# A two-layer encoder: one more couple of seven products in a second wide pair, weight sums in another order, and evictions moved from VectorE to ScalarE

## The chip, the cores and the metric

The kernel runs on one core of a Trainium2 chip. The metric is the device time of one execution in microseconds (us). The engines named here are TensorE (PE: matrix products into PSUM banks of 128 x 512 f32), VectorE (DVE: elementwise), ScalarE (ACT: elementwise, casts, PSUM evictions), GpSimd (POOL) and SyncE (SP: it only issues DMAs here). Each engine works through its own instructions in order; semaphores order the engines among each other.

## The reference

Two layers over 256 tokens of width 2048. The part that the change touches is the second half of each layer, a feed-forward block:

```python
x = x + rms_norm(mixed, g_mix_post)
f = jnp.square(jax.nn.relu(rms_norm(x, g_ffn_pre) @ w_up)) @ w_down   # 2048 -> 8192 -> 2048
return x + rms_norm(f, g_ffn_post)
```

Everything is f32. Ahead of it stand an input projection, dilated window attention with pooling, and an output projection.

## The kernel before, in words

**Products.** An f32 operand is split into a high part (a cast to fp32r on ScalarE) and a low part (the operand less its high part, on VectorE). Every product is then three matmuls into one bank: high by high, high by low, low by high (`three`, L870).

**Weights.** They stream from memory in slots of 128 x 1024 f32 (512 KB). SP loads a slot into one of four `raw` buffers when the low part of what was in that buffer before is made (`load_wide`, L431). ScalarE makes `w_hi` (`split_hi`, L990), VectorE makes `w_lo` (`split_lo`, L1440), both into a ring of eight slots, and TensorE uses them. So one `raw` buffer is bound up from its load to its low part, and the next load into it can't be issued before.

**The feed-forward block** is done in four groups (0 to 3) of 2048 inner columns. A group has four "units" of the up projection (each gives 512 columns for both halves of the tokens, called t = 0 and 1), and then the down projection of those 2048 rows: two "wide pairs" q = 0 and 1, each of 1024 output columns and 16 slots, one slot for each 128 rows (a k tile). Group 3 has one wide pair alone. A plain slot of a wide pair is 12 matmuls: two halves of tokens by two halves of columns by three. 

**Couples.** Two slots next to each other (two k tiles) can be done in one of two ways: as two plain slots, 24 matmuls, or as a couple with seven products in place of eight, 21 matmuls (`seven`, L880; Strassen's scheme in Winograd's form). A couple needs sums of the activations of its two k tiles (`s_sum`, then its high and low part, made once for a group: `s_sums`, `s_rest`) and sums of its weights: three differences `t_sum` of 512 columns and a fourth ("third" in the code) that overwrites the right half of the first slot in `raw`, all on VectorE (`weight_sums`, L1983). ScalarE then makes `t_hi` (1536 columns), VectorE `t_lo`. Four of the seven products gather in four shared banks (`ssa_bank`, two `t_bank`, `o_bank`) over a whole wide pair. After q = 0 VectorE moves these into `kept_sums` (copies in groups 0 and 1, additions in groups 2 and 3: `shared_sums`, L2024), and at the layer's end they are combined into `acc`. The other products gather in the four banks of `acc_pair`, which `wide_sums` (L1946, instructions at L1934 and L1937) adds, scaled by `rstd`, into `acc` after each wide pair.

**Order of work.** It is written out by hand, engine by engine. `SEVEN_AT` says at which slots of a wide pair couples start: 0, 4, 8 and 12, in both pairs. VectorE's order for one couple and its two plain slots is (`seven_lo`, L2017): weight sums, `w_lo` of two slots, `t_lo`, `w_lo` of the two plain slots. ScalarE's is: `w_hi` of the couple's two slots, `t_hi`, `w_hi` of two plain ones; its first cast of a couple waits until "third" has overwritten `raw`. TensorE waits for `w_lo` of a couple's second slot before it starts it, and for `t_lo` some matmuls later. After a second wide pair VectorE makes the low parts of the next unit's first four slots and then evicts the four banks; the next unit's first product waits for the eviction of its bank.

Of the kernel before, what the change touches and what calls it, by code (L numbers as in the profile page):

```python
# [38 lines left out]
F32 = mybir.dt.float32  # L39
# [6 lines left out]
P = 128  # L46
# [96 lines left out]
SHARED = 4  # L143

# [6 lines left out]
def seven_no(l, g, q, n):  # L151

    return ((l * WIDE_LAYER) + g * 2 + q) * len(SEVEN_AT) + n

# [11 lines left out]
def wide_done(l, g, q):  # L166

    return l * WIDE_LAYER + g * 2 + q + 1
# [8 lines left out]
def build(nc, x_in, positions, g_mix_pre, w_in, g_attn_out, w_pool, pool_scale, g_pool_out,  # L177
# [13 lines left out]
    def own(name, shape, dtype=F32):  # L191
# [65 lines left out]
    t_lo = [at(f"t_lo{n}", [P, 3, CH], F32R, low) for n, (_, low) in enumerate(r_t)]  # L257
    r_s = ((r_qkv + 36 * CH, r_qkv + 40 * CH), (r_qkv + 44 * CH, r_xg), (r_xg + 4 * CH, r_post),
           (r_post + 4 * CH, r_post + 8 * CH))
# [26 lines left out]
    rt = [own(f"rt{n}", [P, T, ROPE // 2]) for n in range(6)]  # L286
    rt_i = own("rt_i", [P, T, ROPE // 2], I32)
    pos_f = own("pos_f", [P, T])
    freq = own("freq", [P, ROPE // 2])
# [5 lines left out]
    t_bank = [nc.alloc_psum_tensor(f"t_bank{n}", [P, CH], F32) for n in range(2)]  # L295
    o_bank = nc.alloc_psum_tensor("o_bank", [P, CH], F32)
    ssa_bank = nc.alloc_psum_tensor("ssa_bank", [P, CH], F32)
# [95 lines left out]
    with nc.Block() as block:  # L393
# [3 lines left out]
        def _(sp):  # L397
# [33 lines left out]
            def load_wide(l, g, j, hu):  # L431

                for i in range(SLOTS):
                    p = i % PAIRS

                    sp.wait_ge(lo_made, (hu + i // PAIRS) * PAIRS + p + 1)
                    src = w_down[ld(l, 1), ld(g * D + K_ORDER[i] * P, P), ld(j * 2 * CH, 2 * CH)]
                    sp.dma_start(raw[:, p, :], src.rearrange("a p c -> p (a c)")
                                 ).then_inc(raw_loaded[p], 16)

            def load_group(l, g, last=False):
# [3 lines left out]
                load_wide(l, g, pair_at(g, 0), hu + 2 * CHUNKS)  # L445
                if not last:
                    load_wide(l, g, pair_at(g, 1), hu + 2 * CHUNKS + PAIR_HALVES)
                    return
# [72 lines left out]
        def _(pe):  # L521
# [163 lines left out]
            for l in range(DEPTH):  # L685
# [194 lines left out]
                def seven(g, q, n, hu, result):  # L880

                    i = SEVEN_AT[n]
                    no, s0, s1 = seven_no(l, g, q, n), i % RING, i % RING + 1
                    k0, k1 = K_ORDER[i], K_ORDER[i + 1]
                    first = n == 0
                    begin, end = first and (q == 1 or g == 0), n == len(SEVEN_AT) - 1 and q == 0
# [1524 lines left out]
```

## Time and profile before

| what | before |
|---|---|
| device time, median of 3 runs | 1889.77 us (1889.09 to 1890.19) |
| the profiled execution | 1889.38 us |
| its span, first to last instruction | 1887.3 us |
| TensorE busy | 1874.9 us, 99% |
| VectorE busy | 1497.9 us, 79% |
| ScalarE busy | 1111.4 us, 59% |
| granted TensorE clock, mean | 0.999 |

The profiled execution stands for the runs: it lies 0.4 us below their median. Busy shares are means over the whole span; the down projection's wide pairs are one of several stages, and in them the timelines of the engines are read side by side. In a timeline a length is from start to end of an instruction (or of "x2" of them in a row); the next one of the same engine can start before that end, so the cost of an instruction to its engine is the distance between two starts.

### The profile page before, as it was taken

How to read it: one execution, taken by the hardware profiler on the slowest of the kernel's cores; microseconds unless marked ns; L12 is line 12 of the kernel's file. 1: busy time of each engine (PE TensorE's matmuls, PEld its weight loads, DVE VectorE, ACT ScalarE, POOL GpSimd, SP SyncE). 2: the span in 40 equal slices, each digit the busy share in tenths (PEclk: the TensorE clock that was granted, in tenths of full speed). 3: DMA queues.
4: the chain of work that ended last, by engine and by line, in shares of the span. 5: the costliest groups of instructions: out<-in, count | busy, mean ns of one | idle time of the engine just before them, and what ended most of it. 6: DMA issues, size and time to landing. Idle time of an engine off the chain costs nothing.

```text
span 1887.3 us, 27369 instructions
## 1 busy us (share of the span) xinstructions
PE 1874.9 (99%) x9950; PEld 1672.1 (89%) x9950; DVE 1497.9 (79%) x1885; ACT 1111.4 (59%) x1485; POOL 118.5 (6%) x166
## 2 busy tenths in 40 slices
PE   9999999999999999999999999999999999999998
PEld 7988988988988998898888888889889889989987
DVE  6886657898699689788877757678977996897886
ACT  6455656855665565566554556568556655645662
POOL 3920010000000000000000000100000000000000
PEclk9999999999999999999999999999999999999999
DMA  8665366757566666767576554586676666567673
GB/s 290 201 221 181 112 201 226 236 182 255 189 198 216 214 198 195 236 202 241 210 234 225 187 168 134 170 275 194 197 236 207 195 212 221 183 207 235 221 257 124
DMA packets 170068, 390.92 MB, mean 207 GB/s; under 512 B 12161, under 2 KB 14321, under 8 KB 168433
## 3 DMA queue, kind: packets, MB, share of 16 engines
q1 hardware_dynamic: 167904, 377.58, 61.8%
q10 hardware_dynamic: 2064, 12.08, 1.7%
q8 instruction: 56, 0.92, 0.2%
q14 instruction: 44, 0.35, 0.1%
HBM read 382.53 MB, written 7.08 MB: 206 GB/s over the span
## 4 chain that ended last, share of the span: by engine, by line
PE 95%; DVE 3%; issue 1%; ACT 0%; DMA 0%; POOL 0%; DVEq 0%; POOLq 0%; ACTq 0%
PE acc_pair L573 25%; PE acc_pair L578 13%; PE acc_pair L539 8%; PE acc_pair L540 8%; PE acc_pair L541 8%; PE acc_pair L874 7%; PE acc_pair L873 7%; PE acc_pair L872 7%; DVE w_lo L1445 1%; PE t_bank L874 1%; PE t_bank L873 1%; PE t_bank L872 1%; PE o_bank L791 1%; DVE h_both L1501 1%; PE ssa_bank L872 1%
## 5 line engine op out<-in xcount | busy, mean ns | idle before, releaser
L995 ACT CAST w_hi<-raw 128x1024 fp32r<-128x1024 f32 x687 | 703.6, 1048 | 476.4 <-DVE raw L1998 190.7
L1445 DVE TENSOR_TENSOR w_lo<-raw,w_hi 128x1024 fp32r<-128x1024 f32 x687 | 827.4, 1232 | 169.0 <-ACT w_hi L995 161.8
L573 PE MATMUL acc_pair<-h_both,w_hi 128*128 128x512 f32 x2176 | 560.3, 380 | 0.2
L573 PEld LDWEIGHTS acc_pair<-h_both,w_hi 128*128 128x128 f32 x2176 | 371.4, 190 | 30.4 <-issue 0.5
L578 PEld LDWEIGHTS acc_pair<-h_both,w_lo 128*128 128x128 f32 x2176 | 327.4, 190 | 29.2
L578 PE MATMUL acc_pair<-h_both,w_lo 128*128 128x256 f32 x2176 | 330.5, 274 | 0.0
L872 PE MATMUL acc_pair<-w_hi,f_hi 128*128 128x512 f32 x504 | 191.0, 379 | 0.0
L873 PE MATMUL acc_pair<-w_lo,f_hi 128*128 128x512 f32 x504 | 191.0, 379 | 0.0
L874 PE MATMUL acc_pair<-w_hi,f_lo 128*128 128x512 f32 x504 | 191.0, 379 | 0.0
L539 PE MATMUL acc_pair<-w_hi,h_both 128*128 128x512 f32 x444 | 170.4, 384 | 1.8 <-DVE w_lo L1445 1.6
L540 PE MATMUL acc_pair<-w_lo,h_both 128*128 128x512 f32 x444 | 168.3, 379 | 0.0
L541 PE MATMUL acc_pair<-w_hi,h_both 128*128 128x512 f32 x444 | 168.3, 379 | 0.0
L539 PE MATMUL acc_pair<-w_hi,f_hi 128*128 128x512 f32 x384 | 148.0, 385 | 0.0
L540 PE MATMUL acc_pair<-w_lo,f_hi 128*128 128x512 f32 x384 | 145.5, 379 | 0.0
L541 PE MATMUL acc_pair<-w_hi,f_lo 128*128 128x512 f32 x384 | 145.5, 379 | 0.0
L2013 DVE TENSOR_TENSOR t_lo<-t_sum,t_hi 128x1536 fp32r<-128x1536 f32 x56 | 98.1, 1753 | 12.4 <-ACT t_hi L1325 12.4
L872 PEld LDWEIGHTS acc_pair<-w_hi,f_hi 128*128 128x128 f32 x504 | 95.3, 189 | 13.5
L874 PEld LDWEIGHTS acc_pair<-w_hi,f_lo 128*128 128x128 f32 x504 | 95.3, 189 | 13.5
L873 PEld LDWEIGHTS acc_pair<-w_lo,f_hi 128*128 128x128 f32 x504 | 95.3, 189 | 13.5
L2223 POOL TENSOR_TENSOR rstd<-mean_sq,minus_half 128x1 f32<-128x1 f32 (+1 forms) x16 | 13.5, 843 | 1407.8 <-DVE ss_post L1460 1135.5
L539 PEld LDWEIGHTS acc_pair<-w_hi,h_both 128*128 128x128 f32 x444 | 83.9, 189 | 15.7 <-issue 2.9
L541 PEld LDWEIGHTS acc_pair<-w_hi,h_both 128*128 128x128 f32 x444 | 83.9, 189 | 12.0
(252 smaller groups left out, 2293.8 us busy)
## 6 DMA issues: line engine op xcount, KB each, us to landing
raw<-in_w_up SPq DMA_DIRECT2D x256, 512.0 KB, 4.4
raw<-in_w_down SPq DMA_DIRECT2D x240, 512.0 KB, 5.0
raw<-in_w_in SPq DMA_DIRECT2D x128, 512.0 KB, 4.7
raw<-in_w_out SPq DMA_DIRECT2D x64, 512.0 KB, 5.3
raw_side<-in_w_down SPq DMA_DIRECT2D x16, 512.0 KB, 7.0
x_kept<-x ACTq DMA_DIRECT2D x4, 1024.0 KB, 6.2
x<-x_kept ACTq DMA_DIRECT2D x4, 1024.0 KB, 6.1
x<-in_x SPq DMA_DIRECT2D x8, 256.0 KB, 7.5
```

The lines of the kernel that those rows point to most:

```text
L539: pe.matmul(bank[:, :], xh, wh, start=begin and k == 0, stop=False)
L540: pe.matmul(bank[:, :], xh, wl, start=False, stop=False)
L541: mm = pe.matmul(bank[:, :], xl, wh, start=False, stop=end and k == 1)
L573: pe.matmul(acc_pair[b][:, m, :], w_hi[:, slot, col:col + P], x_both.rearrange("p s (a n) -> p s n a", a=2), start=(slot, k) == (0, 0), st ...
L578: mm = pe.matmul(acc_pair[b][:, m, 0:SEQ], w_lo[:, slot, col:col + P], x_hi.rearrange("p (a n) -> p n a", a=2), start=False, stop=(slot, k ...
L791: mm = pe.matmul(o_bank[:, e * SEQ:(e + 1) * SEQ], proj[:, 6 + h // 4, kt, h_cols(h % 4)], probs_t[:, e, kt, :], start=kt == 0, stop=kt == 1)
L872: pe.matmul(bank, xh, in_turn(wh), start=start, stop=False)
L873: pe.matmul(bank, xh, in_turn(wl), start=False, stop=False)
L874: return pe.matmul(bank, xl, in_turn(wh), start=False, stop=stop)
L995: act.copy(w_hi[:, half * PAIRS + p, :], raw[:, p, :]).then_inc(hi_made, 1)
L1445: dve.tensor_tensor(w_lo[:, slot, :], src[:, p, :], w_hi[:, slot, :].bitcast(F32), ALU.subtract).then_inc(lo_made, 1)
L2013: dve.tensor_tensor(t_lo[n % 2][:, :, :], t_sum[n % 2][:, :, :], t_hi[n % 2][:, :, :].bitcast(F32), ALU.subtract).then_inc(t_lo_made, 1)
```

## The change

- The second wide pair of groups 0 to 2 has five couples, at slots 0, 4, 8, 12 and 14; its k tiles come in another order. The first wide pair is as it was.
- There is a fifth set of activation sums, made in the last unit of each group.
- "Third" is now the first of the weight sums and waits for both slots to be loaded; then one sum of 512 columns, then one subtraction of 1024 columns in place of two of 512. The third of the fifth couple stands ahead of `t_lo` of the fourth.
- The four shared banks are one PSUM tensor. In groups 2 and 3 VectorE adds them with one instruction of 2048 columns, in groups 0 and 1 ScalarE copies them.
- In group 0 ScalarE evicts `acc_pair` into `acc` after both wide pairs, in place of VectorE.
- After a second wide pair VectorE evicts behind two `w_lo` of the next unit, not four.
- Some small tables share memory with a buffer.

```diff
-SEVEN_AT = (0, PAIRS, RING, RING + PAIRS)
-SEVEN_UNIT = ((1, 0), (1, 1), (2, 0), (2, 1))
-K_ORDER = (4, 5, 0, 1, 6, 7, 2, 3, 8, 9, 12, 13, 10, 11, 14, 15)
+SEVEN_AT = ((0, 4, 8, 12), (0, 4, 8, 12, 14))
+COUPLES = tuple(len(at) for at in SEVEN_AT)
+SEVEN_UNIT = ((1, 0), (1, 1), (2, 0), (2, 1), (3, 0))[:max(COUPLES)]
...
+                def first_shared(g):
+
+                    if g == 0:
+                        act.wait_ge(x_saved, 16 * T * (l + 1))
+                    act.wait_ge(t_used, 3 * seven_no(l, g, 0, COUPLES[0]) - 1)
+                    for k in range(SHARED):
+                        act.copy(kept_sums[:, 1 - pair_at(g, 0), k, :], shared[:, k, :]
+                                 ).then_inc(shared_free, 1)
...
                     if not last:
-                        for n in range(PAIR_HALVES):
-                            seven_hi(g, 1, n, hu + 12 + n, n % 2)
-                        split_hi(hu + 16, 0)
+                        wide_hi(g, 1, 0, 2)
+                        if g < T:
+                            first_shared(g)
+                        two_hi(g, 1, 2)
+                        if first:
+                            first_sums(0)
+                        wide_hi(g, 1, 4)
+                        split_hi(hu + 16, 0, (0, 1))
+                        if first:
+                            first_sums(1)
+                        split_hi(hu + 16, 0, (2, 3))
                         split_hi(hu + 17, 1)
                         return
...
-                def weight_sums(g, q, n, hu):
...
-                    dve.wait_ge(raw_loaded[0], hu * 16 + 16)
-                    dve.tensor_tensor(out[:, 0, :], top_r, top_l, ALU.subtract
-                                      ).then_inc(t_step, 1)
-                    dve.wait_ge(raw_loaded[1], hu * 16 + 16)
-                    dve.tensor_tensor(top_r, low_r, top_r, ALU.subtract).then_inc(t_third, 1)
...
-                    dve.tensor_tensor(out[:, 1, :], low_r, out[:, 0, :], ALU.subtract
-                                      ).then_inc(t_step, 1)
...
-                    dve.tensor_tensor(out[:, 2, :], low_l, out[:, 1, :], ALU.subtract
-                                      ).then_inc(t_step, 1)
+                def weight_third(g, q, n):
...
+                    for m in range(2):
+                        dve.wait_ge(raw_loaded[i % PAIRS + m], hu * 16 + 16)
+                    dve.tensor_tensor(top_r, low_r, top_r, ALU.subtract).then_inc(t_third, 1)
+
+                def weight_sums(g, q, n):
...
+                    dve.wait_ge(t_third, no + 1)
+                    dve.tensor_tensor(out[:, 0, :], top[:, c_cols(1)], top[:, c_cols(0)], ALU.add
                                       ).then_inc(t_step, 1)
...
+                    dve.tensor_tensor(out[:, 1:3, :], low, out[:, 0:1, :].to_broadcast([P, 2, CH]),
+                                      ALU.subtract).then_inc(t_step, 1)
...
+                    dst = kept_sums[:, 1 - pair_at(g, 0), :, :]
+                    dve.tensor_tensor(dst, shared[:, :, :], dst, ALU.add
+                                      ).then_inc(shared_free, SHARED)
```

**Where instructions move.** The first place is VectorE, the end of the second wide pair of group 1, from the last couple's weight sums on. In the names, `t_sum_94` and the like are buffers. Before:

```order
L1995 TENSOR_TENSOR t_sum_94<-raw 128x512 [waits raw_loaded0,t_used]
L1998 TENSOR_TENSOR raw<-raw 128x512 [waits raw_loaded1]
L2002 TENSOR_TENSOR t_sum_94<-raw,t_sum_94 128x512 [waits t_used,t_step]
L2007 TENSOR_TENSOR t_sum_94<-raw,t_sum_94 128x512 [waits t_used,t_step]
L1445 TENSOR_TENSOR w_lo<-raw,w_hi 128x1024 [waits hi_made] x2
L2013 TENSOR_TENSOR t_lo_96<-t_sum_94,t_hi_92 128x1536 [waits t_hi_made]
L1445 TENSOR_TENSOR w_lo<-raw,w_hi 128x1024 [waits hi_made] x6
L1937 SCALAR_TENSOR_TENSOR acc<-acc_pair,rstd,acc 128x512 [waits acc_done] x2
L1937 SCALAR_TENSOR_TENSOR acc<-acc_pair,rstd,acc 128x512 [waits third_done]
L1937 SCALAR_TENSOR_TENSOR acc<-acc_pair,rstd,acc 128x512 [waits w_used]
```

After, from the weight sums of the fourth couple of that pair:

```order
L2083 TENSOR_TENSOR t_sum_94<-raw 128x512 [waits t_third,t_used]
L2088 TENSOR_TENSOR t_sum_94<-raw,t_sum_94 128x1024 [waits t_used,t_step]
L1522 TENSOR_TENSOR w_lo<-raw,w_hi 128x1024 [waits hi_made] x2
L2068 TENSOR_TENSOR raw<-raw 128x512 [waits raw_loaded3,raw_loaded2]
L2095 TENSOR_TENSOR t_lo_96<-t_sum_94,t_hi_92 128x1536 [waits t_hi_made]
L2083 TENSOR_TENSOR t_sum_93<-raw 128x512 [waits t_third,t_used]
L2088 TENSOR_TENSOR t_sum_93<-raw,t_sum_93 128x1024 [waits t_used,t_step]
L1522 TENSOR_TENSOR w_lo<-raw,w_hi 128x1024 [waits hi_made] x2
L2095 TENSOR_TENSOR t_lo_95<-t_sum_93,t_hi_91 128x1536 [waits t_hi_made]
L1522 TENSOR_TENSOR w_lo<-raw,w_hi 128x1024 [waits hi_made] x2
L2009 SCALAR_TENSOR_TENSOR acc<-acc_pair,rstd,acc 128x512 [waits acc_done,acc_free0]
L2009 SCALAR_TENSOR_TENSOR acc<-acc_pair,rstd,acc 128x512 [waits w_used]
```

The fifth couple (third, `t_sum_93`, two `w_lo`, `t_lo_95`) stands in the place of two plain `w_lo`, and the four evictions come after two of the next unit's `w_lo` in place of four.

The second place is ScalarE, the end of the second wide pair of group 0 and the start of group 1's first unit. Before:

```order
L1325 CAST t_hi_92<-t_sum_94 128x1536 [waits t_step]
L995 CAST w_hi<-raw 128x1024 [waits w_used,raw_loaded2]
L995 CAST w_hi<-raw 128x1024 [waits w_used,raw_loaded3]
L995 CAST w_hi<-raw 128x1024 [waits w_used,raw_loaded0]
L995 CAST w_hi<-raw 128x1024 [waits w_used,raw_loaded1]
L995 CAST w_hi<-raw 128x1024 [waits w_used,raw_loaded2]
```

After:

```order
L1389 CAST t_hi_91<-t_sum_93 128x1536 [waits t_step]
L1022 CAST w_hi<-raw 128x1024 [waits w_used,raw_loaded0]
L1022 CAST w_hi<-raw 128x1024 [waits w_used,raw_loaded1]
L1380 ACTIVATE acc<-acc_pair,rstd 128x512 [waits acc_done,rstd_ready]
L1380 ACTIVATE acc<-acc_pair,rstd 128x512 [waits w_used]
L1380 ACTIVATE acc<-acc_pair,rstd 128x512 [waits t_used]
L1380 ACTIVATE acc<-acc_pair,rstd 128x512
L1022 CAST w_hi<-raw 128x1024 [waits w_used,raw_loaded2]
L1022 CAST w_hi<-raw 128x1024 [waits w_used,raw_loaded3]
```

There is one more `t_hi`, and four evictions (L1380) stand between the casts of slots 1 and 2 of the next unit.

The third place is VectorE in the last unit of group 1, between two uses of `acc_pair` by L1914 (after: L1991). Before:

```order
L1914 TENSOR_TENSOR act_f<-acc_pair,act_f 128x512 [waits half_taken]
L1995 TENSOR_TENSOR t_sum_94<-raw 128x512 [waits raw_loaded0,t_used]
L1998 TENSOR_TENSOR raw<-raw 128x512 [waits raw_loaded1]
L2002 TENSOR_TENSOR t_sum_94<-raw,t_sum_94 128x512 [waits t_used,t_step]
L2007 TENSOR_TENSOR t_sum_94<-raw,t_sum_94 128x512 [waits t_used,t_step]
L1924 TENSOR_TENSOR f_lo<-act_f,f_hi 128x512 [waits fhi_made,f_ready]
L1445 TENSOR_TENSOR w_lo<-raw,w_hi 128x1024 [waits hi_made] x2
L1914 TENSOR_TENSOR act_f<-acc_pair,act_f 128x512 [waits half_taken]
```

After:

```order
L1991 TENSOR_TENSOR act_f<-acc_pair,act_f 128x512 [waits half_taken]
L2068 TENSOR_TENSOR raw<-raw 128x512 [waits raw_loaded1,raw_loaded0]
L2083 TENSOR_TENSOR t_sum_94<-raw 128x512 [waits t_third,t_used]
L2088 TENSOR_TENSOR t_sum_94<-raw,t_sum_94 128x1024 [waits t_step]
L2043 TENSOR_TENSOR s_sum_106<-act_f 128x128 [waits f_ready]
L2045 TENSOR_TENSOR s_sum_106<-act_f 128x128
L2048 TENSOR_TENSOR s_sum_106<-s_sum_106,act_f 128x128 [waits s_step]
L2051 TENSOR_TENSOR s_sum_106<-act_f,s_sum_106 128x128 [waits s_step]
L2001 TENSOR_TENSOR f_lo<-act_f,f_hi 128x512 [waits fhi_made]
L1522 TENSOR_TENSOR w_lo<-raw,w_hi 128x1024 [waits hi_made] x2
L1991 TENSOR_TENSOR act_f<-acc_pair,act_f 128x512 [waits half_taken]
```

The two differences that were one after the other are one, and four small additions (`s_sum_106`) come ahead of `f_lo`, which ScalarE waits for before it makes `t_hi` of the second couple.

## Rows read from the trace of the kernel before

**Rows 1.** Page, part 1: busy us (share of the span), instructions of each engine.
```profile
PE 1874.9 (99%) x9950; PEld 1672.1 (89%) x9950; DVE 1497.9 (79%) x1885; ACT 1111.4 (59%) x1485; POOL 118.5 (6%) x166
```
**Rows 2.** Timeline of TensorE, group 1, layer 0: start and length (us), line, tiles.
```profile
543.69 0.38 PE L872 MATMUL acc_pair<-t_hi,f_hi 128*128 128x512 f32 x1
...
588.37 0.38 PE L872 MATMUL ssa_bank<-w_hi,s_hi 128*128 128x512 f32 x1
...
598.08 0.38 PE L872 MATMUL ssa_bank<-w_hi,s_hi 128*128 128x512 f32 x1
...
617.50 1.03 PE L573 MATMUL acc_pair<-h_both,w_hi 128*128 128x512 f32 x4
...
618.81 1.03 PE L573 MATMUL acc_pair<-h_both,w_hi 128*128 128x512 f32 x4
```
**Rows 3.** Timeline of VectorE, same stage; in brackets idle time before, and releaser.
```profile
541.39 0.68 DVE L1914 TENSOR_TENSOR act_f<-acc_pair,act_f 128x512 f32<-128x512 f32 x1
...
546.65 1.76 DVE L2013 TENSOR_TENSOR t_lo<-t_sum,t_hi 128x1536 fp32r<-128x1536 f32 x1 [1.54 <-ACT t_hi L1325]
...
550.86 2.35 DVE L1445 TENSOR_TENSOR w_lo<-raw,w_hi 128x1024 fp32r<-128x1024 f32 x2
553.13 1.75 DVE L2013 TENSOR_TENSOR t_lo<-t_sum,t_hi 128x1536 fp32r<-128x1536 f32 x1
554.80 2.35 DVE L1445 TENSOR_TENSOR w_lo<-raw,w_hi 128x1024 fp32r<-128x1024 f32 x2
557.07 0.68 DVE L1995 TENSOR_TENSOR t_sum<-raw 128x512 f32<-128x512 f32 x1
558.06 0.69 DVE L1998 TENSOR_TENSOR raw<-raw 128x512 f32<-128x512 f32 x1 [0.31 <-DMA raw<-in_w_down]
558.67 0.68 DVE L2002 TENSOR_TENSOR t_sum<-raw,t_sum 128x512 f32<-128x512 f32 x1
559.39 0.69 DVE L2007 TENSOR_TENSOR t_sum<-raw,t_sum 128x512 f32<-128x512 f32 x1
560.00 2.35 DVE L1445 TENSOR_TENSOR w_lo<-raw,w_hi 128x1024 fp32r<-128x1024 f32 x2
...
577.95 2.71 DVE L1937 SCALAR_TENSOR_TENSOR acc<-acc_pair,rstd,acc 128x512 f32<-128x512 f32 x4
...
583.11 2.35 DVE L1445 TENSOR_TENSOR w_lo<-raw,w_hi 128x1024 fp32r<-128x1024 f32 x2
...
592.21 2.35 DVE L1445 TENSOR_TENSOR w_lo<-raw,w_hi 128x1024 fp32r<-128x1024 f32 x2
...
599.70 0.69 DVE L1998 TENSOR_TENSOR raw<-raw 128x512 f32<-128x512 f32 x1 [0.59 <-DMA raw<-in_w_down]
```
**Rows 4.** Waits of VectorE: total us, times, longest.
```profile
DVE raw L1998 <- DMA raw<-in_w_down: 10.1, 24, 0.8
```
**Rows 5.** Timeline of VectorE, four small additions of one sum of activations, group 1.
```profile
517.44 0.29 DVE L1965 TENSOR_TENSOR s_sum<-act_f 128x128 f32<-128x128 f32 x1
...
518.50 0.68 DVE L1924 TENSOR_TENSOR f_lo<-act_f,f_hi 128x512 fp32r<-128x512 f32 x1
```
**Rows 6.** Groups of instructions by line and form: total us, mean ns.
```profile
L995 ACT CAST w_hi<-raw 128x1024 fp32r<-128x1024 f32 x687 | 703.6, 1048 | 476.4 <-DVE raw L1998 190.7 <-PE acc_pair L578 94.1 <-PE acc_pair L541 73.2
...
L1292 ACT COPY act_f<-acc_pair 128x512 f32<-128x512 f32 x60 | 35.0, 584 | 95.0 <-PE acc_pair L578 94.7
...
L1223 ACT ACTIVATE acc<-acc_pair,rstd 128x512 f32<-128x512 f32 x16 | 11.0, 685 | 3.0 <-PE acc_pair L541 3.0
...
L2035 DVE TENSOR_TENSOR kept_sums<-t_bank,kept_sums 128x512 f32<-128x512 f32 x8 | 5.1, 680 | 0.0
```
**Rows 7.** Timeline of both engines where group 2 of layer 0 ends.
```profile
777.74 2.72 DVE L1937 SCALAR_TENSOR_TENSOR acc<-acc_pair,rstd,acc 128x512 f32<-128x512 f32 x4
...
778.83 0.38 PE L874 MATMUL acc_pair<-w_hi,f_lo 128*128 128x512 f32 x1
...
779.29 1.12 PE L573 MATMUL acc_pair<-h_both,w_hi 128*128 128x512 f32 x4
```

More of the change, by code:

```diff
@@ L137, with k_order, t_buffer @@
 WIDE_LAYER = 2 * FF_GROUPS - 1
-SEVEN_AT = (0, PAIRS, RING, RING + PAIRS)
-SEVEN_UNIT = ((1, 0), (1, 1), (2, 0), (2, 1))
-K_ORDER = (4, 5, 0, 1, 6, 7, 2, 3, 8, 9, 12, 13, 10, 11, 14, 15)
+SEVEN_AT = ((0, 4, 8, 12), (0, 4, 8, 12, 14))
+COUPLES = tuple(len(at) for at in SEVEN_AT)
+LAYER_COUPLES = FF_GROUPS * COUPLES[0] + (FF_GROUPS - 1) * COUPLES[1]
+SEVEN_UNIT = ((1, 0), (1, 1), (2, 0), (2, 1), (3, 0))[:max(COUPLES)]
 SHARED = 4
+def k_order(q):
+    pairs = [4 * u + 2 * b for u, b in SEVEN_UNIT[:COUPLES[q]]]
+    plain, order = iter([k for k in range(0, KT, 2) if k not in pairs]), []
+    for i in range(0, SLOTS, 2):
+        k = pairs[SEVEN_AT[q].index(i)] if i in SEVEN_AT[q] else next(plain)
+        order += [k, k + 1]
+    return order
+K_ORDER = (k_order(0), k_order(1))
+def t_buffer(q, n):
+    return (q * COUPLES[0] + n) % 2
 def pair_at(g, q):
@@ L151, in seven_no @@
 def seven_no(l, g, q, n):
-    return ((l * WIDE_LAYER) + g * 2 + q) * len(SEVEN_AT) + n
+    return l * LAYER_COUPLES + g * sum(COUPLES) + q * COUPLES[0] + n
 def shared_done(l, g):
@@ L294, in build @@
     s_bank = [pair[:, 1, :] for pair in acc_pair]
-    t_bank = [nc.alloc_psum_tensor(f"t_bank{n}", [P, CH], F32) for n in range(2)]
-    o_bank = nc.alloc_psum_tensor("o_bank", [P, CH], F32)
-    ssa_bank = nc.alloc_psum_tensor("ssa_bank", [P, CH], F32)
+    shared = nc.alloc_psum_tensor("shared", [P, SHARED, CH], F32)
+    ssa_bank, t_bank, o_bank = shared[:, 0, :], [shared[:, 1, :], shared[:, 2, :]], shared[:, 3, :]
     sem = nc.alloc_semaphore
@@ new lines, in wide_hi @@
+                def wide_hi(g, q, begin, end=SLOTS):
+                    for i in range(begin, end, 2):
+                        two_hi(g, q, i)
+                        if i in SEVEN_AT[q]:
+                            sums_hi(g, q, SEVEN_AT[q].index(i))
+                def first_shared(g):
[5 more added lines that the diff above has]
+                                 ).then_inc(shared_free, 1)
@@ L2012, in sums_lo @@
                     dve.wait_ge(t_hi_made, seven_no(l, g, q, n) + 1)
[L2013 to L2014 removed]
+                    dve.tensor_tensor(low[:, :, :], t_sum[t_buffer(q, n)][:, :, :],
+                                      high[:, :, :].bitcast(F32), ALU.subtract
                                       ).then_inc(t_lo_made, 1)
[L2017 to L2022 removed]
@@ new lines, in couple_lo, with wide_lo @@
+                def couple_lo(g, q, i):
+                    n = SEVEN_AT[q].index(i)
+                    weight_sums(g, q, n)
+                    two_lo(g, q, i)
+                    if i + 2 in SEVEN_AT[q]:
+                        weight_third(g, q, n + 1)
+                    sums_lo(g, q, n)
+                def wide_lo(g, q, begin):
+                    for i in range(begin, SLOTS, 2):
+                        if i not in SEVEN_AT[q]:
+                            two_lo(g, q, i)
+                            continue
+                        if i - 2 not in SEVEN_AT[q]:
+                            weight_third(g, q, SEVEN_AT[q].index(i))
+                        couple_lo(g, q, i)
```

256 lines of the change are left out of this document (145 added, 111 removed).

## The prediction

> **What bounds the kernel now.** I read the page first: TensorE is busy 99% of the span [rows 1], so time goes down only as matmuls go and up only as TensorE is made to stop. In the timeline of the second wide pair of group 1, layer 0, couples of four slots start 9.71 us apart, 45 matmuls each (21 of the couple, 24 of its two plain slots), so one 512-column matmul takes 9.71/45 = 0.2158 us [rows 2]. The question is then how far ahead of TensorE its suppliers are. The timeline of VectorE gives that: a couple can start when the low part of its second slot is made, and TensorE starts 588.37 - (583.11 + 2.35) = 2.91 us after that at slot 4, and 598.08 - (592.21 + 2.35) = 3.52 us after it at slot 8 [rows 2, 3]. VectorE gains about 0.6 us per couple, and then spends it: 2.71 us of evictions per pair [rows 3]. I call this number the lead; the change spends it.
>
> The loop that sets VectorE's pace is one of latency. A slot is reloaded when its low part is made. The part of the couple's second slot ended at 550.86 + 2.35 = 553.21, and its next contents let L1998 go at 558.06: 4.85 us [rows 3]. At 592.21 + 2.35 = 594.56 and 599.70 it is 5.14 [rows 3]; I take 4.97, the mean of the four such places in this group's wide stage. L1998 waited so in 24 of its 56 runs, 10.1 us in all [rows 4]: four couples a group, in three groups and two layers.
>
> **The change part by part.** *Matmuls.* A couple is 21 matmuls where two plain slots are 24. Three groups in each of two layers get one more couple: 6 x 3 = 18 fewer, 18 x 0.2158 = 3.88 us, all on TensorE's path.
>
> *Order of the weight sums.* Before: four sums of 512 columns, the first done ahead of the second slot's landing (557.07 did not wait, 558.06 did). From landing to the end of the second low part: 560.00 + 2.35 - 558.06 = 4.29 us [rows 3]. After, the third difference comes first and waits for both landings, and the other two instructions each need the one ahead. A sum that needs the one ahead follows after 0.72 (558.67 to 559.39), otherwise after 0.60 [rows 3]. A subtraction of 1024 columns is issued in about 2.27/2 = 1.14 (560.00 plus two low parts to the next instruction; the same spacing follows from 550.86 to 553.13) [rows 3]. So 0.72 + 0.72 + 1.14 = 2.58 in place of 0.60 + 0.60 + 0.72 + 0.61 = 2.53: no gain, and all of it stands behind the landing. From landing to the second low part: 2.58 + 2.35 = 4.93, so 0.64 later at each couple that waits for its landing. The cycle becomes 4.97 + 4.93 = 9.90 us against TensorE's 9.71: the lead now shrinks by 0.19 a cycle instead of growing.
>
> The Trainium skill, "VectorE: DVE Perf Modes", section on the TRN2 errata, gives an fp32 tensor_tensor (N + 151)/0.96 ns, 691 at 512 columns, which the 0.68 to 0.69 of the rows agrees with [rows 3]. By it two subtractions in one save 158 ns a couple; eight couples would give the tightest place 8 x (0.158 + 0.05) = 1.7 us more lead, and the time would be near the second rival's. The rows speak against it: durations overlap there, and what counts is the spacing, 0.60 and 1.14, which saves 0.06, and a second handover of 0.12 eats it.
>
> *A fifth sum of activations* in each group's last unit: four small additions, 518.50 - 517.44 = 1.06 us of VectorE, and a low part of 0.60 [rows 5]. The instructions behind it are delayed by 1.06. TensorE uses the bank that L1914 frees: that ended at 541.39 + 0.68 = 542.07 and TensorE comes at 543.69, so 1.62 shrinks to 0.56 [rows 2, 3], hidden, but nearly not. The t_lo at 546.65 waits 1.54 for ScalarE, which waits for f_lo of the same unit [rows 3]; so most of the 1.06 gets through, and I take 1.0. The low part of 0.60 stands in that wait.
>
> *The lag at slot 4 of the second pair*: 1.0, and 0.05 and 0.64 and 0.64 for three couples, and 0.05 for its own sums: 2.38. Three groups then differ.
> Group 2: the shared banks are added by one instruction of 2048 columns. No row shows one; three rows of 512, 1024 and 1536 are spaced 0.60, 1.14 and 1.67 (553.13 to 554.80) [rows 3], so 2.2, against four of 0.60. Bounds are 1.67 and 2.72 (four rows of 0.680 [rows 6]). It gains 0.2. Lead: 2.91 - 2.38 + 0.2 = 0.73, then 0.54, then 0.35.
> Group 1: ScalarE copies the shared banks, four of 0.584 [rows 6], right behind t_hi. VectorE is spared 2.40, but its next low parts wait for casts that stand behind the copies: from the third difference on ScalarE needs about 7.1 (two casts, t_hi, four copies, a cast, less overlaps) where VectorE needs 6.5, so 0.6 comes back. Lead: 0.73 - 0.2 + 1.8 = 2.33, 2.14, 1.95.
> Group 0: as group 1, and the four evictions of 2.71 go to ScalarE too [rows 3]. Lead above 4.
>
> *The fifth couple* has no plain slots behind it. From the end of the fourth couple's low parts VectorE needs the third difference (0.60), t_lo (1.67), the add (0.72), the subtraction (1.14) and two low parts (2.27): 6.40. TensorE has 21 matmuls, 4.53. The lead falls by 1.87: to -1.52 in group 2, 0.08 in group 1, above 2 in group 0. A stop adds handover and a slow start: the second of four evictions ended at 777.74 + 2.72 - 1.32 = 779.14, TensorE went on at 779.29, and its first four matmuls took 1.12 where 1.03 is usual [rows 2, 7]: 0.15 + 0.09 = 0.24. Group 2 stops for 1.52 + 0.24 = 1.76, group 1 for 0.16.
>
> *The evictions behind it.* Before, they wait for TensorE (779.29 is the one stop of this kind, 0.34, and it goes) [rows 7]. Now t_lo of the fifth couple (1.67), two low parts (2.27) and two evictions (1.32) end 5.26 after the low part that let TensorE go; with 0.15 the next unit can start at 5.41, and TensorE is there at 0.24 + 4.53 = 4.77. Stop 0.64, with the slow start 0.73, in groups 1 and 2.
> Group 0: ScalarE evicts all four between the casts of slots 1 and 2 of the next unit. The last product is there 0.38 - 0.22 = 0.16 after TensorE could go on, then two evictions 2 x 0.685 less 0.10 of overlap, a cast 1.05 [rows 6], a low part 1.23 (half of 2.35 and a little): 3.71. TensorE wants the third slot 2 x 1.31 = 2.62 later (617.50 to 618.81 for one) [rows 2]. Stop 1.09 + 0.24 = 1.33.
>
> *At no cost*: group 3's fifth sum, in the same last unit, and no fifth couple there: its lag of 2.3 stands against the lead of 2.9. If that cover is short, group 3 costs up to 1 us a layer. Tables moved in memory and the order of k tiles change addresses alone; SP's queue waits for the same low parts.
>
> **Sum.** Per layer 1.33 + (0.16 + 0.73) + (1.76 + 0.73) = 4.71, two layers 9.42. Against the profiled execution of 1889.38 us (a span of 1887.3 and 2.1 around it; 0.4 under the median of the runs, 1889.77): 1889.38 - 3.88 - 0.34 + 9.42 = 1894.6.
>
> **Rivals.** *The stops don't come*: if the evictions and copies given to ScalarE leave VectorE ahead everywhere, 1889.38 - 3.88 - 0.34 = 1885.2. For it: VectorE gains 0.6 a couple now, and 2.4 to 5.1 us of its work a pair go elsewhere in half of the groups. Against it: 6.40 against 4.53 at the fifth couple, and group 0's stop, which rests on no lead at all. Chance 0.13.
> *The lead holds*: landings at 4.5 us, since the transfers meet fewer others. Four waiting landings a group give 4 x 0.47 = 1.9. Group 2's lead at the fifth couple is then +0.36, its eviction stop 5.41 - 0.36 - 4.53 + 0.09 = 0.6, group 1 has none, group 0 keeps 1.33: 1885.2 + 2 x 1.93 = 1889.1, no change. It decides from a landing of about 4.6. Against it: 4.85 to 5.14 in the rows [rows 3]. Chance 0.25. The Trainium skill's rule on one wide instruction would come out near here too, by another way; I give that 0.05, as the spacing in the rows is against it. Together 0.30.
> *Landings come later*, because loads of the fifth couple and of the next unit now crowd: each 0.1 us costs groups 1 and 2 of both layers 4 x 0.4 = 1.6; at 5.27 it is 1899.4. Chance 0.12.
>
> **Numbers.** The forecast has 0.45. Under 0.2% (3.78 us) I call no change, which is about what a measurement of this kernel can tell. The forecast lies 1.1 above that bound and its own sizes are good to 2 or 3 us, so a fourth of it falls in no change: slower 0.34 + 0.12 and some of the second rival's upper side, 0.52; no change 0.35; faster 0.13. The range, 1886.5 to 1899.5, takes in the bounds on the shared add (0.5 either way, two layers: 1), and the second and last rivals; it leaves about 0.1 below and 0.1 above. The forecast's own range is 1891.5 to 1898.
>
> **What would show it.** Right: TensorE stops in front of the fifth couple (its first product of ssa_bank) for about 1.8 us in group 2 and hardly in group 1; in front of a unit's first product for 0.7 in groups 1 and 2; at the third slot of group 1's first unit (behind group 0) for 1.3; idle VectorE of about 1 us in front of the third difference, by DMA. Wrong: an idle time of that kind under 0.6, a lead in group 2 that holds above 0.7 at slot 12, or stops that fall elsewhere, such as in front of the bank that L1914's place frees.

## The result, and the profile after

The changed kernel takes 1899.11 us (median of 5 runs, 1898.06 to 1900.44) against 1889.88 us before in the same series: a ratio of 1.0049, 95% interval 1.0034 to 1.0063, so 9.2 us slower. The forecast was 1894.6, slower by about 5; the time lies at the upper end of the range (1886.5 to 1899.5) and above the forecast's own (1891.5 to 1898).

The profiled execution took 1899.60 us, 0.5 more than the median. Its span grew from 1887.3 to 1897.5 us, by 10.2, although TensorE has 9932 matmuls where it had 9950 [rows 1]. The waits of TensorE, after (engine, line, what it waited for: total us, times, longest; L595 is the first product of an up projection's slot, L894 the first of a couple's three):

```profile
PE shared L894 <- DVE w_lo L1522: 5.0, 4, 1.9
PE acc_pair L595 <- DVE acc L2009: 2.2, 4, 0.6
PE acc_pair L595 <- DVE w_lo L1522: 1.9, 2, 0.9
```

Before, the feed-forward blocks had a single stop, of 0.35 us [rows 7]. The first line is the stop in front of couples, the second that for evictions, the third that of group 1's first unit at its third slot. They tell waits alone; a stop also has a handover. So I added up over the whole trace by how much the distance of two matmul starts exceeds the usual one for their width: in the feed-forward blocks 0.35 us before and 13.36 after, elsewhere 9.48 and 10.57. 13.36 - 0.35 + 1.09 - 3.88 = 10.2, the whole of the span's growth. Of the 1.09 elsewhere, 1.08 lie in the first 50 us, and they are scatter rather than the change: the first product of L595 (L573 before) starts at 33.54 us before and at 34.42 here, but at 34.07 and 34.04 in two more traces of the same changed kernel, and anywhere from 33.47 to 34.48 in those of the experiments.

Timeline of TensorE after, layer 0, at the places that the prediction named:

```profile
460.16 1.13 PE L595 MATMUL acc_pair<-h_both,w_hi 128*128 128x512 f32 x4 [0.93 <-DVE w_lo L1522]
...
590.05 0.38 PE L894 MATMUL shared<-w_hi,s_hi 128*128 128x512 f32 x1
...
599.76 0.38 PE L894 MATMUL shared<-w_hi,s_hi 128*128 128x512 f32 x1
...
609.48 0.38 PE L894 MATMUL shared<-w_hi,s_hi 128*128 128x512 f32 x1
...
614.53 0.48 PE L894 MATMUL shared<-w_hi,s_hi 128*128 128x512 f32 x1 [0.36 <-DVE w_lo L1522]
...
619.89 1.13 PE L595 MATMUL acc_pair<-h_both,w_hi 128*128 128x512 f32 x4 [0.56 <-DVE acc L2009]
...
778.95 0.48 PE L894 MATMUL shared<-w_hi,s_hi 128*128 128x512 f32 x1 [1.92 <-DVE w_lo L1522]
...
784.31 1.12 PE L595 MATMUL acc_pair<-h_both,w_hi 128*128 128x512 f32 x4 [0.56 <-DVE acc L2009]
```

460.16 is the third slot of group 1's first unit (group 0's evictions), 614.53 and 778.95 are fifth couples of groups 1 and 2, 619.89 and 784.31 the first products of the units behind them. Each stop is followed by a first matmul of 0.48 or a first four of 1.12 or 1.13.

Timeline of VectorE after, second wide pair of group 1 (L2068 is third, L2083 the sum, L2088 the wide subtraction, L2095 t_lo, L1522 a low part, L2009 an eviction):

```profile
585.49 2.35 DVE L1522 TENSOR_TENSOR w_lo<-raw,w_hi 128x1024 fp32r<-128x1024 f32 x2
...
593.07 0.69 DVE L2068 TENSOR_TENSOR raw<-raw 128x512 f32<-128x512 f32 x1 [1.29 <-DMA raw<-in_w_down]
593.87 0.69 DVE L2083 TENSOR_TENSOR t_sum<-raw 128x512 f32<-128x512 f32 x1
594.60 1.23 DVE L2088 TENSOR_TENSOR t_sum<-raw,t_sum 128x1024 f32<-128x1024 f32 x1
595.74 2.35 DVE L1522 TENSOR_TENSOR w_lo<-raw,w_hi 128x1024 fp32r<-128x1024 f32 x2
...
605.61 2.35 DVE L1522 TENSOR_TENSOR w_lo<-raw,w_hi 128x1024 fp32r<-128x1024 f32 x2
607.98 0.69 DVE L2068 TENSOR_TENSOR raw<-raw 128x512 f32<-128x512 f32 x1
608.59 1.75 DVE L2095 TENSOR_TENSOR t_lo<-t_sum,t_hi 128x1536 fp32r<-128x1536 f32 x1
610.26 0.68 DVE L2083 TENSOR_TENSOR t_sum<-raw 128x512 f32<-128x512 f32 x1
610.98 1.22 DVE L2088 TENSOR_TENSOR t_sum<-raw,t_sum 128x1024 f32<-128x1024 f32 x1
612.12 2.35 DVE L1522 TENSOR_TENSOR w_lo<-raw,w_hi 128x1024 fp32r<-128x1024 f32 x2
614.39 1.75 DVE L2095 TENSOR_TENSOR t_lo<-t_sum,t_hi 128x1536 fp32r<-128x1536 f32 x1
616.06 2.35 DVE L1522 TENSOR_TENSOR w_lo<-raw,w_hi 128x1024 fp32r<-128x1024 f32 x2
618.33 2.72 DVE L2009 SCALAR_TENSOR_TENSOR acc<-acc_pair,rstd,acc 128x512 f32<-128x512 f32 x4
```

The lead, from these two timelines: 590.05 - (585.49 + 2.35) = 2.21 us at slot 4, 599.76 - (595.74 + 2.35) = 1.67 at slot 8, 609.48 - (605.61 + 2.35) = 1.52 at slot 12, and at slot 14 TensorE starts 0.06 after the low part. Before it grew in this place, from 2.91 to 3.52 [rows 2, 3]. Third waits 1.29 for its landing at 593.07, where VectorE used to do one of its sums. Over the trace these waits are:

```profile
DVE raw L2068 <- DMA raw<-in_w_down: 29.8, 30, 1.6
```

That is 0.99 us each, against 10.1 us in 24 waits [rows 4].

### The profile page after: what moved, and what is told of

Its sections match the earlier page's. It is cut to its first block, busy times and chain, and to the rows that moved or that the text cites. A ratio compares the mean times of both kernels' runs of the same rounds, so it can differ in the third digit from the quotient of the medians.

```text
span 1897.5 us, 27369 instructions
## 1 busy us (share of the span) xinstructions
PE 1876.2 (99%) x9932; PEld 1668.0 (88%) x9932; DVE 1513.9 (80%) x1849; ACT 1145.6 (60%) x1531; POOL 117.6 (6%) x166
## 4 chain that ended last, share of the span: by engine, by line
PE 84%; DVE 10%; DMA 3%; issue 2%; ACT 1%; POOL 0%; DVEq 0%; POOLq 0%; ACTq 0%; SPq 0%
PE acc_pair L595 24%; PE acc_pair L600 12%; PE acc_pair L561 8%; PE acc_pair L563 8%; PE acc_pair L562 8%; PE acc_pair L894 5%; PE acc_pair L896 5%; PE acc_pair L895 5%; DVE w_lo L1522 4%; DMA raw<-in_w_down 3%; PE shared L894 2%; PE shared L896 2%; PE shared L895 2%; DVE t_sum L2088 1%; PE shared L813 1%
## 5 line engine op out<-in xcount | busy, mean ns | idle before, releaser
L1522 DVE TENSOR_TENSOR w_lo<-raw,w_hi 128x1024 fp32r<-128x1024 f32 x687 | 827.5, 1232 | 168.2 <-ACT w_hi L1022 161.1
L595 PE MATMUL acc_pair<-h_both,w_hi 128*128 128x512 f32 x2176 | 560.9, 380 | 4.2 <-DVE acc L2009 2.2
L595 PEld LDWEIGHTS acc_pair<-h_both,w_hi 128*128 128x128 f32 x2176 | 371.2, 190 | 35.8 <-issue 3.8
L894 PE MATMUL acc_pair<-w_hi,f_hi 128*128 128x512 f32 x462 | 175.3, 379 | 0.0
L895 PE MATMUL acc_pair<-w_lo,f_hi 128*128 128x512 f32 x462 | 175.1, 379 | 0.0
L896 PE MATMUL acc_pair<-w_hi,f_lo 128*128 128x512 f32 x462 | 175.1, 379 | 0.0
L561 PE MATMUL acc_pair<-w_hi,f_hi 128*128 128x512 f32 x384 | 148.0, 385 | 0.0
L562 PE MATMUL acc_pair<-w_lo,f_hi 128*128 128x512 f32 x384 | 145.5, 379 | 0.0
L563 PE MATMUL acc_pair<-w_hi,f_lo 128*128 128x512 f32 x384 | 145.5, 379 | 0.0
L2095 DVE TENSOR_TENSOR t_lo<-t_sum,t_hi 128x1536 fp32r<-128x1536 f32 x62 | 108.6, 1752 | 7.9 <-ACT t_hi L1389 7.9
L1389 ACT CAST t_hi<-t_sum 128x1536 fp32r<-128x1536 f32 x62 | 91.6, 1478 | 15.4 <-DVE t_sum L2088 9.2
L894 PEld LDWEIGHTS acc_pair<-w_hi,f_hi 128*128 128x128 f32 x462 | 87.3, 189 | 13.1 <-DVE acc L2009 0.7
L896 PEld LDWEIGHTS acc_pair<-w_hi,f_lo 128*128 128x128 f32 x462 | 87.3, 189 | 12.4
L895 PEld LDWEIGHTS acc_pair<-w_lo,f_hi 128*128 128x128 f32 x462 | 87.3, 189 | 12.4
L561 PEld LDWEIGHTS acc_pair<-w_hi,h_both 128*128 128x128 f32 x444 | 83.9, 189 | 15.8 <-issue 3.0
```

The source lines that it names most:

```text
L561: pe.matmul(bank[:, :], xh, wh, start=begin and k == 0, stop=False)
L562: pe.matmul(bank[:, :], xh, wl, start=False, stop=False)
L563: mm = pe.matmul(bank[:, :], xl, wh, start=False, stop=end and k == 1)
L595: pe.matmul(acc_pair[b][:, m, :], w_hi[:, slot, col:col + P], x_both.rearrange("p s (a n) -> p s n a", a=2), start=(slot, k) == (0, 0), st ...
L894: pe.matmul(bank, xh, in_turn(wh), start=start, stop=False)
L895: pe.matmul(bank, xh, in_turn(wl), start=False, stop=False)
```

## The experiments

Theory A is the prediction's: the new order of the weight sums makes VectorE's loop of landing, sums and low parts longer than TensorE's cycle, the fifth couple then falls on a lead that is nearly used up, and evictions stand ahead of low parts that TensorE wants. Theory B: the fifth couple alone is too dense for VectorE. Theory C: ScalarE's added copies and evictions delay the casts. There were three series, each on another chip; kernels of one series share their runs of the kernel before (medians 1890.10, 1889.72 and 1889.92 us). The changed kernel itself was not run in the first of them, so differences to it from there are good to 2 or 3 us (one kernel below moved by 2.4 us from one series to another). In the edits, "..." stands for lines left out: names, counts and waits that only follow.

**Four couples again.**

```diff
-SEVEN_AT = ((0, 4, 8, 12), (0, 4, 8, 12, 14))
+SEVEN_AT = ((0, 4, 8, 12), (0, 4, 8, 12))
...
```

(With it the evictions wait for a plain last slot again, and the fifth set of activation sums goes too, as `SEVEN_UNIT` is as long as the larger number of couples.)

> The changed kernel with four couples in the second wide pair, as before; all else as changed (weight sums with third first, ScalarE's copies and evictions). 18 matmuls come back: +3.88 us. Theory A (the order of the weight sums puts VectorE's loop behind TensorE's, and the fifth couple falls on a lead that is used up): the stops in front of slot 14 (0.62, 2.18, 1.35, 1.86) and the eviction stops behind (4 x 0.82) go, but third still waits about 0.9 us for its landing at each couple, and the lead still falls from couple to couple; group 0's 2 x 1.2 stay. About 1893 us. Theory B (the fifth couple alone is too dense, 6.4 us of VectorE against 4.5 of TensorE; the order of the sums matters little): leads as in the kernel before, growing from couple to couple, only group 0's stop left, 1892. The time hardly tells them apart, the leads do.

1890.49 us (1889.85 to 1891.42), ratio 1.0003 (0.9994 to 1.0013). The time is below both expectations: group 0's stops are shorter, and smaller stops that the expectation left out, 1.67 us in all, go with the others but for 0.14. What TensorE still waits for is group 0's evictions, at 0.62 us in place of 1.20, twice:

```profile
PE acc_pair L595 <- DVE w_lo L1518: 0.7, 2, 0.4
```

The leads, at slots 4, 8 and 12 of the second pair, go with theory A: in group 1 of layer 0 they are 2.39, 1.99, 1.91, in group 2 of layer 1 0.74, 0.23, 0.08, where the kernel before had 2.77, 3.34, 3.93 in the latter. In the other two they hold rather than fall (2.63, 2.58, 2.52 in group 2 of layer 0; 2.39, 2.88, 2.18 in group 1 of layer 1, with landings down to 4.2 us among them), but in neither do they grow through the pair as before. Third waits for its landing as in the changed kernel, 25.6 us in 28 waits. The order takes away the lead's growth by itself, and four couples are just few enough that the lead lasts to the end of the pair. 1899.1 - 1890.5 = 8.6 us, across series, is what the fifth couple and its activation sums cost on top of that order; they save 3.9 in matmuls, so they bring stops of about 12.5 (in the traces the stops fall from 13.36 to 1.38).

**The old order of the weight sums, five couples.**

```diff
 weight_third:
...
+    dve.wait_ge(raw_loaded[i % PAIRS], hu * 16 + 16)
+    dve.tensor_tensor(out[:, 2, :], top_r, top_l, ALU.subtract).then_inc(t_step, 1)
+    dve.wait_ge(raw_loaded[i % PAIRS + 1], hu * 16 + 16)
     dve.tensor_tensor(top_r, low_r, top_r, ALU.subtract).then_inc(t_third, 1)
 weight_sums:
...
-    dve.tensor_tensor(out[:, 0, :], top[:, c_cols(1)], top[:, c_cols(0)], ALU.add ...
-    dve.tensor_tensor(out[:, 1:3, :], low, out[:, 0:1, :].to_broadcast([P, 2, CH]), ...
+    dve.tensor_tensor(out[:, 0, :], low_r, out[:, 2, :], ALU.subtract ...
+    dve.tensor_tensor(out[:, 1, :], low_l, out[:, 0, :], ALU.subtract ...
```

> The changed kernel, five couples, with the old order of the weight sums: one difference of the first slot ahead of third, then two of 512 columns. Theory A: the first difference is done while VectorE would wait for the second slot, third to second low part takes 0.6 us less per couple, leads grow again, group 2 has about 1 us in hand at slot 14: all stops in front of couples go, and most of the eviction stops; only group 0's 2.4 are left. 1888.5 us (1887.5 to 1890). Theory B: VectorE's 6.4 against 4.5 at the fifth couple is as before, stops of about 1.5 to 2 us stay in groups 1 and 2: 1896 to 1898. Theory C (ScalarE's added work delays the casts): no change, 1899.

1889.37 us (1888.62 to 1890.16), ratio 0.9997 (0.9987 to 1.0007). Theory B falls, and theory C with it for all but group 0's two stops: no stop in front of any couple is left, with the same fifth couples and ScalarE's added work. In group 1 of layer 0 the lead is 2.52, 3.49, 4.06 and 1.67 at slot 14, in group 2 2.05, 3.02, 3.71 and 1.77. So the fifth couple still takes 1.9 to 2.4 us of lead, where the prediction had 1.87; with the old order there is a lead to take it from. VectorE in that stage (L2075 is the difference of the first slot):

```profile
599.13 0.69 DVE L2075 TENSOR_TENSOR t_sum<-raw 128x512 f32<-128x512 f32 x1
600.12 0.69 DVE L2077 TENSOR_TENSOR raw<-raw 128x512 f32<-128x512 f32 x1 [0.31 <-DMA raw<-in_w_down]
600.73 0.69 DVE L2085 TENSOR_TENSOR t_sum<-raw,t_sum 128x512 f32<-128x512 f32 x1
601.45 0.69 DVE L2090 TENSOR_TENSOR t_sum<-raw,t_sum 128x512 f32<-128x512 f32 x1
602.06 2.35 DVE L1522 TENSOR_TENSOR w_lo<-raw,w_hi 128x1024 fp32r<-128x1024 f32 x2
...
617.81 1.41 DVE L2009 SCALAR_TENSOR_TENSOR acc<-acc_pair,rstd,acc 128x512 f32<-128x512 f32 x2 [1.18 <-PE acc_pair L896]
619.13 4.62 DVE L1522 TENSOR_TENSOR w_lo<-raw,w_hi 128x1024 fp32r<-128x1024 f32 x4
```

599.13 needs the first slot alone and fills most of the wait; from landing (600.12) to the end of the second low part (602.06 + 2.35) it takes 4.29, as before. All waits of third:

```profile
DVE raw L2077 <- DMA raw<-in_w_down: 9.2, 21, 0.8
```

What is left: the two stops of 1.20 at group 1's first unit,

```profile
PE acc_pair L595 <- DVE w_lo L1522: 1.9, 2, 0.9
```

and four of 0.35 that are read off the rows at 617.81 and 619.13: the evictions of t = 1 wait for TensorE's last product, and the low part of the next unit's third slot stands behind them. In the changed kernel VectorE was later than TensorE there, so it was the evictions that were late.

**One eviction moved at a time.** In group 0:

```diff
...
                         split_hi(hu + 16, 0, (0, 1))
                         if first:
-                            first_sums(1)
+                            first_sums(1, (0,))
                         split_hi(hu + 16, 0, (2, 3))
+                        if first:
+                            first_sums(1, (1,))
```

> The changed kernel; in group 0 ScalarE evicts the two banks of t = 1 of the second pair behind the casts of slots 2 and 3 of the next unit, not ahead of them. Theory A: the two stops of 1.2 us at the third slot of group 1's first unit go, nothing else moves: 1896.7 us. Theory C (ScalarE's added work is what costs most): more than that goes, since later casts come earlier too: 1895 or less.

In groups 1 and 2:

```diff
...
-                        split_lo(nxt, 0, (0, 1))
+                        split_lo(nxt, 0, (0,))
                         if not first:
-                            wide_sums(g, q)
-                        split_lo(nxt, 0, (2, 3))
+                            wide_sums(g, q, (0,))
+                        split_lo(nxt, 0, (1, 2, 3))
+                        if not first:
+                            wide_sums(g, q, (1,))
```

> The changed kernel; in groups 1 and 2 VectorE evicts the banks of t = 0 behind one low part of the next unit and those of t = 1 behind four, in place of all behind two. Theory A: the first product of the next unit waits for two evictions that come one low part (1.14 us) earlier, so the four stops of 0.82 us at 619.90, 784.32, 1560.02 and 1724.46 go, and those of the couples stay: 1899.1 - 3.3 = 1895.8 us. If low parts of the next unit are then late in their place (the second slot is wanted 1.31 us after the first), up to 1 us of it comes back.

1894.21 (1891.59 to 1895.55) and 1894.24 us (1891.11 to 1896.41): both faster than expected. In the first, the waits for low parts at L595 are gone and those for evictions are there; in the second it is the other way round:

```profile
PE shared L894 <- DVE w_lo L1524: 3.8, 3, 1.6
PE acc_pair L595 <- DVE acc L2011: 2.2, 4, 0.6
```

```profile
PE shared L894 <- DVE w_lo L1522: 4.4, 5, 1.9
PE acc_pair L595 <- DVE w_lo L1522: 1.9, 2, 0.9
```

So of the two kinds of eviction stop each move takes away its own alone. The rest of the gain had to be the series or a second effect. Both were run again beside the changed kernel, which had meanwhile been at 1899.36 (1898.61 to 1899.93) in another series; on that run was expected:

> The changed kernel, unaltered. The moves of evictions alone gave 1894.2 each, 2.5 and 1.6 us less than the stops that they take away explain. If landings differ from one series of runs to the next, the changed kernel itself is at about 1897 here, with its stops in front of slot 14 shorter and the others the same. If those moves have a second effect, it is at 1899 again.

It was at 1899 again, which by that text speaks for a second effect; but the moves had run in the first series, on another chip. In one series:

> The changed kernel, unaltered, beside the two runs of one moved eviction each, to see the three in one series: 1899.2 us, as twice before.

> The changed kernel with group 0's evictions of t = 1 behind the casts of slots 2 and 3, again. Theory A (only the two stops of 1.2 go, the rest of the earlier 4.9 was the series): 1896.8 us. If the move has a second effect, 1894.2 again.

> The changed kernel with the evictions of groups 1 and 2 split around the next unit's low parts, again. Theory A (only the four stops of 0.82 go): 1895.9 us. If the move has a second effect, 1894.2 again.

The changed kernel took 1898.17 us (1897.34 to 1898.86), group 0's move 1896.63 (1894.49 to 1898.83), that of groups 1 and 2 1895.10 (1894.14 to 1896.83): 1.5 and 3.1 us less, where theory A expects 2.4 and 3.3, and the five runs of the first move spread over 4.3 us. There is no second effect of the size that the first series showed. The same kernel moved from 1894.21 to 1896.63 between series, more than the kernel before did. The traces point at the landings: where third waits in groups 1 and 2, they take a mean of 4.94 us in the first and 5.01 in the second trace of this kernel, and 4.99 and 5.04 in the two of the other move. At the prediction's price for later landings (1.6 us for 0.1) that is an estimated 1 us each, of the 2.4 and 0.9 by which the medians moved; with one trace each, the rest stays open.

**Both moves, without the old order.** (Edit: the two above.)

> The changed kernel with both moves of evictions, and its own order of the weight sums. Theory A: the two stops of 1.2 and the four of 0.82 go and those in front of the couples stay, 1899.1 - 2.4 - 3.3 = 1893.4 us. If the two moves took away 4.9 us each, as their own runs against the first time of the changed kernel say, 1889.5.

1892.73 us (1890.32 to 1894.71), 6.6 less than the changed kernel in the same series, where 5.7 was expected. 8.5 us of stops are left in its trace, all in front of couples but for 0.2 in group 3 and 0.3 inside a first couple of group 2, of a kind that the next section tells of.

**The wide subtraction as two narrow ones.**

```diff
-    dve.tensor_tensor(out[:, 1:3, :], low, out[:, 0:1, :].to_broadcast([P, 2, CH]), ALU.subtract)
+    dve.tensor_tensor(out[:, 1, :], low[:, 0, :], out[:, 0, :], ALU.subtract)
+    dve.tensor_tensor(out[:, 2, :], low[:, 1, :], out[:, 0, :], ALU.subtract)
```

> The changed kernel with the subtraction of 1024 columns as two of 512, in the same place and order. By the spacing in rows (0.60 and 0.60 against 1.14) each couple takes 0.06 us longer on VectorE; by durations that add up (two of 0.691 against one of 1.224) 0.16 longer. The stop in front of slot 14 in group 2 sums what eight couples lose: 0.5 us more by the first, 1.3 by the second, and as much in group 1. Time 1900 to 1901 by the first, 1903 to 1904 by the second.

1901.07 us, 1.7 above the changed kernel of its series, from two runs only, so the time alone shows little. VectorE:

```profile
561.11 0.69 DVE L2068 TENSOR_TENSOR raw<-raw 128x512 f32<-128x512 f32 x1 [1.17 <-DMA raw<-in_w_down]
561.90 0.69 DVE L2083 TENSOR_TENSOR t_sum<-raw 128x512 f32<-128x512 f32 x1
562.63 0.69 DVE L2088 TENSOR_TENSOR t_sum<-raw,t_sum 128x512 f32<-128x512 f32 x1
563.24 0.69 DVE L2089 TENSOR_TENSOR t_sum<-raw,t_sum 128x512 f32<-128x512 f32 x1
563.84 2.36 DVE L1522 TENSOR_TENSOR w_lo<-raw,w_hi 128x1024 fp32r<-128x1024 f32 x2
```

The two take 563.84 - 562.63 = 1.21 in place of 595.74 - 594.60 = 1.14: 0.07 a couple, the spacing and not the sum of durations. The Trainium skill's figures for durations ("VectorE: DVE Perf Modes", section on the TRN2 errata) agree with the rows, 0.69, but what a merged instruction saves here is less than half of what they give.

**All three.** (Edit: old order, both moves of evictions.)

> The changed kernel with all three: the old order of the weight sums, group 0's evictions of t = 1 behind the casts of slots 2 and 3, and in groups 1 and 2 the evictions of t = 0 behind one low part and of t = 1 behind four. Theory A: the run with the old order alone had only two stops of 1.20 us and four of 0.35 us left in the two feed-forward blocks; both kinds go, so 1889.4 - 2.4 - 1.4 = 1885.6 us, which is 0.2% under the kernel before and its 18 matmuls. Rival: a supplier is late in a new place, since evictions that come earlier push low parts of the next unit back; then 1887 to 1888.

1885.21 us (1884.60 to 1886.36), ratio to before 0.9975 (0.9966 to 0.9985): 4.5 us faster than the kernel before, and 14 faster than the changed kernel in its series. TensorE waits for nothing in the feed-forward blocks; what is left lies outside them:

```profile
PE shared L641 <- POOL ident L2357: 1.8, 1, 1.8
PE acc_pair L561 <- DVE w_lo L1524: 1.2, 3, 0.4
PE acc_pair L646 <- DMA rows_mix<-in_g_mix_pre: 0.3, 1, 0.3
PE shared L657 <- DMA x<-in_x: 0.2, 1, 0.2
```

## Why the prediction was right, and which size was off

The direction, the three places of the large stops and their cause were right, and theory A stood against two rivals. The size was off: the stops came to 13.36 us where 9.42 were forecast. That the time still lies in the range is in part luck, as its upper end was drawn for a rival, later landings, that explains only a part of the miss. The profiled execution missed by 1899.6 - 1894.6 = 5.0 us. Step by step, in layer 0 and layer 1:

- *Group 0's evictions*: forecast 1.33 a layer, found 1.20 and 1.20.
- *Eviction stops behind the fifth couple*: forecast 0.73, found 0.82 four times.
- *Stops in front of couples*: forecast 0.16 in group 1 and 1.76 in group 2, so 3.84 in all. Found 0.62 and 1.35 in group 1, 2.18 and 1.86 at slot 14 in group 2, and 0.81 at earlier couples of group 2 which I had at a small positive lead: 6.82. This is the term that was mis-sized, by 2.98 of the 5.0.
- *Put at nothing*: 0.16 and 0.30 inside the first couple of group 2's second pair, in front of the first bank that VectorE evicts behind the shared add, and 0.40 once in group 3. Another 1.09 is the scatter at the start.

The two kinds that were put at nothing, at TensorE's loading of weights (PEld) for the product that waits:

```profile
744.52 2.72 DVE L2009 SCALAR_TENSOR_TENSOR acc<-acc_pair,rstd,acc 128x512 f32<-128x512 f32 x4
745.32 0.19 PEld L894 LDWEIGHTS acc_pair<-w_hi,f_hi 128*128 128x128 f32 x1 [0.29 <-DVE acc L2009]
...
1811.85 0.68 DVE L1991 TENSOR_TENSOR act_f<-acc_pair,act_f 128x512 f32<-128x512 f32 x1
1812.58 0.19 PEld L894 LDWEIGHTS acc_pair<-t_hi,f_hi 128*128 128x128 f32 x1 [0.54 <-DVE act_f L1991]
```

The second is the bank of L1991, L1914 before, which the prediction named as a sign of being wrong. It came once: the fifth sum had left 0.56 us there, and one late landing (third waited 0.59) used it up.

The mechanism of the mis-sized term was right, its sums too small in three ways, all in the same direction. First, the sum behind third came 0.80 after it (593.07 to 593.87), not the 0.72 that I read between two other dependent sums; the chain from landing to the second low part is 595.74 + 2.35 - 593.07 = 5.02, not 4.93. Second, landings where third waits in groups 1 and 2 of both layers took a mean of 5.04 us (4.66 to 5.50), not 4.97. Third, the fifth couple's stretch is 612.12 - 605.61 = 6.51, not 6.40. At the prediction's own price (0.1 us in the loop costs 1.6) the first is an estimated 1.4 us and the second 1.2; the third, four times, is 0.4: 3.0 together, about what is missing. No lead stood against them in group 2, where it was 0.40 and not 0.73 at slot 4, and 0.06 from slot 8 on.

Group 0's lead was forecast too large as well: 0.99 and 1.31 at slot 14 where I had above 2. It costs nothing in this trace, but TensorE stopped there for 0.18 and 0.48 us in one layer of two later traces, of the changed kernel and of group 0's move. And rows 4 were read wrongly: of the 24 waits two lie in group 3 (at 881.50 and 1816.84), so it isn't four in each of the other groups. The sum does not use it.

What was sized well: the delay from the fifth sum of activations, put at 1.0 (the lead at slot 4 of group 2's first pair is 6.86 us here and 7.92 with four couples, where that sum is gone); the shared add of 2048 columns, of which no row stood before, 742.25 - 740.05 = 2.20, as estimated:

```profile
740.05 2.28 DVE L2128 TENSOR_TENSOR kept_sums<-shared,kept_sums 128x2048 f32<-128x2048 f32 x1
742.25 2.35 DVE L1522 TENSOR_TENSOR w_lo<-raw,w_hi 128x1024 fp32r<-128x1024 f32 x2
```

and the wait of third, "about 1 us", found 0.99. The rival of later landings (1899.4) is nearest to the time that was measured, but by its cause only in part: it needed 5.27, and landings were at 5.04, against 4.98 where third waited in these places before. The rival of a lead that holds asked for 4.6.

Why the sum behind third starts 0.08 later than another dependent sum, the trace can tell. In the first couple of all it doesn't:

```profile
365.21 0.68 DVE L2068 TENSOR_TENSOR raw<-raw 128x512 f32<-128x512 f32 x1
365.93 0.69 DVE L2083 TENSOR_TENSOR t_sum<-raw 128x512 f32<-128x512 f32 x1
```

There it is 0.72, although third wrote in place there too. What differs is the waits: in the first couple the sum waits for third alone, in all others for a second semaphore as well (`t_used`, once `tables_saved`), and then the wait for third is an instruction of its own in the trace (EVENT_SEMAPHORE, L2082, in 61 of 62 couples), ahead of a sum that carries the other wait. In all ten traces with this order the spacing is 0.72 in that one couple, and 0.78 to 0.80 in all 55 others where the sum stands right behind third. The subtraction behind it carries its own wait for the sum, and follows after 0.72 or 0.73. That the order of the two waits is the cause was not tried apart.

## What to carry to other kernels

When a buffer's reload waits for its last reader, the loop is landing latency plus everything that stands behind the landing; work that needs only what landed earlier is free inside that wait, and moving it behind the landing lengthens the loop by its whole duration, even where the number of instructions falls. Ask of such a loop whether the lead of the supplier grows or shrinks per cycle: once it shrinks, every tenth of a microsecond by which the loop was taken too short is paid again in each cycle, so that small errors of reading become large ones of the forecast. Evictions that wait for a last product belong behind the low parts that the next stage wants first, bank by bank.

## What the runs showed of the hardware

Distances between starts on VectorE, 128 partitions of f32: 0.60 for 512 columns, 1.14 for 1024, 1.67 for 1536, 2.20 for 2048: 0.07 and 0.53 for each 512, so merging saves 0.07 an instruction. One that needs its predecessor's result starts 0.12 later, and 0.18 to 0.20 later where the wait for that result is an instruction of its own ahead of it (593.07 to 593.87). After each stop TensorE's first matmul of a couple takes 0.48 in place of 0.38.
